# Scan stage: the mean square of a head as two split products in place of one unsplit product

## The reference

```
o = (gla_chunked(q, k_f, v, lf_f)
     + flip_t(gla_chunked(flip_t(q), flip_t(k_b), flip_t(v), flip_t(lf_b))))
o = rmsnorm(o, norm_g.reshape(HG_HEADS, HG_VAL_DIM)).reshape(bsz, t, HG_W).astype(u.dtype)
o = o * jax.nn.silu(gate)
return jnp.concatenate([o, memory_cross_attn(xq, mem_kv)], axis=-1) @ w_out
```

## Time and profile before

| | |
|---|---|
| runs | 1357.15, 1355.12, 1357.15 us, median 1357.15 |
| profiled execution | 1358.22 us, of which the span from first to last instruction is 1356.9 |
| mean granted TensorE clock | 0.996 of full |
| scan stage loop | about 1009 to 1161 us of the span |
| busy: PE / PEld / DVE / ACT / POOL | 98% / 86% / 75% / 58% / 11% |

### The profile page before, as it was taken

How to read it: one execution, slowest core, us unless ns; L and a number is a source line. 1 busy time by engine, 2 the same in 40 slices (tenths; PEclk the granted TensorE clock), 3 DMA queues, 4 the chain that set the end, 5 groups by cost and what they waited for, 6 DMA issues and landing times. The chain is left out here.

```text
span 1356.9 us, 20744 instructions
## 1 busy us (share of the span) xinstructions
PE 1334.4 (98%) x8197; PEld 1160.9 (86%) x8197; DVE 1023.1 (75%) x1670; ACT 785.7 (58%) x1274; POOL 145.0 (11%) x131
## 2 busy tenths in 40 slices
PE   8999999999999999999999999999999999999998
PEld 7887888888898888887987888888789998888887
DVE  5875588777897787778788677766657997786766
ACT  6654266655442566563687565555557785655553
POOL 4760300000100000000000000000303224000000
PEclk9999999999999999999999999999999999999999
DMA  8722355654563456552643255555344435355551
GB/s 304 244 85 119 111 200 217 234 188 184 194 249 125 186 188 251 195 197 101 234 147 119 112 205 199 225 196 187 135 179 153 149 138 189 146 187 205 194 197 70
DMA packets 38607, 242.18 MB, mean 178 GB/s; under 512 B 4448, under 2 KB 7408, under 8 KB 11120
## 3 DMA queue, kind: packets, MB, share of 16 engines
q1 hardware_dynamic: 38512, 240.87, 48.2%
HBM read 236.89 MB, written 2.64 MB: 177 GB/s over the span
## 5 line engine op out<-in xcount | busy, mean ns | idle before, releaser
L320 DVE TENSOR_TENSOR wlo<-raw,whi 128x2048 fp32r<-128x2048 f32 (+1 forms) x179 | 401.2, 2246 | 103.8 <-ACT whi L297 101.7
L297 ACT ACTIVATE whi<-raw 128x2048 fp32r<-128x2048 f32 x195 | 370.4, 1903 | 81.3 <-PE ps L472 40.0
L409 PE MATMUL ps<-XS,whi 128*128 128x512 f32 x1392 | 331.7, 390 | 0.0
L409 PEld LDWEIGHTS ps<-XS,whi 128*128 128x128 f32 x1392 | 257.9, 188 | 52.0 <-issue 0.6
L461 PE MATMUL ps<-whi,MS 128*128 128x512 f32 x960 | 233.5, 391 | 0.0
L461 PEld LDWEIGHTS ps<-whi,MS 128*128 128x128 f32 x960 | 177.5, 188 | 35.8 <-issue 0.4
L414 PEld LDWEIGHTS ps<-XS,wlo 128*128 128x128 f32 x1392 | 178.5, 191 | 6.8
L414 PE MATMUL ps<-XS,wlo 128*128 128x256 f32 x1392 | 180.6, 283 | 0.0
L389 PE MATMUL ps<-XS,whi 128*128 128x256 f32 x672 | 167.8, 289 | 0.0
L390 PE MATMUL ps<-XS,whi 128*128 128x256 f32 x672 | 164.1, 284 | 0.0
L1563 ACT ACTIVATE ar<-ps 128x256 f32<-128x256 f32 x176 | 57.3, 377 | 146.3 <-PE ps L414 146.1
(11 more groups left out here) (328 smaller groups left out, 1548.4 us busy)
## 6 DMA issues: line engine op xcount, KB each, us to landing
raw<-in_up SPq DMA_DIRECT2D x88, 1024.0 KB, 4.8
raw<-in_down SPq DMA_DIRECT2D x44, 1024.0 KB, 4.9
raw<-in_hg_t SPq DMA_DIRECT2D x16, 1024.0 KB, 4.8
raw<-in_od_t SPq DMA_DIRECT2D x8, 1024.0 KB, 5.2
raw<-in_ev_a SPq DMA_DIRECT2D x6, 1024.0 KB, 10.0
raw<-in_wa_o SPq DMA_DIRECT2D x6, 1024.0 KB, 4.9
raw<-in_hg_o SPq DMA_DIRECT2D x6, 1024.0 KB, 4.8
raw<-in_ev_o SPq DMA_DIRECT2D x4, 1024.0 KB, 6.8
```

Of the source, the lines that this page charges most:

```text
L297: ac.activation(parts_of(m)[0][:, 0:w], raw[m % NRAW][:, 0:w], ACT.Copy).then_inc(w_hi)
L320: ve.tensor_tensor(lo[:, c], r[:, c], hi[:, c].bitcast(F32), ALU.subtract).then_inc(w_lo_v)
L409: pe.matmul(banks[i][:, 0:512], hi[:, c], XS[:, k, 0:512], start=(k == 0), stop=False)
```

## The change

The squares of heads 0 to 6 are summed in split form. ScalarE makes the high part of the square, VectorE the low part; they use chunk 7 of `MS`. The matrix of ones is copied once into chunk 6 in the float32r format. TensorE then makes two products where it made one. Head 7 stays as before. In TensorE's order the squares of head n-2 come behind the scores of head n-1. Square also waits until the low part of the head before is made.

```
+        h_one, h_sh, h_sl = mark("h_one"), mark("h_sh"), mark("h_sl")
+        ONES, SRS = MS[:, 6, 0:128], MS[:, 7, :]
...
+                if 0 <= n - 1 < 8:
+                    scores_pe(n - 1)
                 if 0 <= n - 2 < 8:
                     squares_pe(n - 2)
-                if 0 <= n - 1 < 8:
-                    scores_pe(n - 1)
...
         def squares_pe(h):
-            pe.wait_ge(h_sr.sem, h + 1)
             if h:
                 pe.wait_ge(h_rs.sem, h)
-            pe.matmul(HSUM[:, 0:256], C("ones")[:, 0:128], SR, start=True, stop=True).then_inc(h_su.up())
+            if h == 7:
+                pe.wait_ge(h_sr.sem, h + 1)
+                pe.matmul(HSUM[:, 0:256], C("ones")[:, 0:128], SR, start=True, stop=True).then_inc(h_su.up())
+                return
+            pe.wait_ge(h_one.sem, 1)
+            pe.wait_ge(h_sh.sem, h + 1)
+            pe.matmul(HSUM[:, 0:256], ONES, SRS[:, 0:256], start=True, stop=False)
+            pe.wait_ge(h_sl.sem, h + 1)
+            pe.matmul(HSUM[:, 0:256], ONES, SRS[:, 256:512], start=False, stop=True).then_inc(h_su.up())
...
+            ac.activation(ONES, C("ones")[:, 0:128], ACT.Copy).then_inc(h_one.up())
             act_weights(at_z(1))
...
                     if h:
                         ac.wait_ge(h_su.sem, h)
+                        ac.wait_ge(h_sl.sem, h)
                     ac.activation(SR, HVAL[:, 0:256], ACT.Square).then_inc(h_sr.up())
+                    if h < 7:
+                        ac.wait_ge(h_sr.sem, h + 1)
+                        ac.activation(SRS[:, 0:256], SR, ACT.Copy).then_inc(h_sh.up())
...
                     ve.scalar_tensor_tensor(UG[h % 2], HVAL[:, 0:256], col("bng", h), GT[h % 2], ALU.mult,
                                             ALU.mult).then_inc(h_ug.up())
+                    if h < 7:
+                        ve.wait_ge(h_sh.sem, h + 1)
+                        ve.tensor_tensor(SRS[:, 256:512], SR, SRS[:, 0:256].bitcast(F32), ALU.subtract).then_inc(h_sl.up())
```

## The result

The changed kernel's median is 1362.98 us (6 runs, 1361.76 to 1364.85), the kernel before's 1356.24. The ratio is 1.0049, 95% interval 1.0038 to 1.0059: 6.7 us slower (5.2 to 8.0). A second series gave 1.0043 (1.0029 to 1.0057). The profiled execution took 1363.35 us, span 1361.9, against 1358.22 and 1356.9: 5.1 us longer.

A forecast was written before the change was run, and what follows sets the result against it. The prediction took the ScalarE–VectorE ring, not TensorE, to bound the scan stage. It summed 1.15 + 1.9 + 0.58 = 3.6 us to a median of 1360.8 us (profiled 1361.8), 80% range 1357.6 to 1363.2.

The forecast's parts named there:

- What bounds the stage: Scan stage: ScalarE and VectorE waiting on each other set its end at 14.70 us a turn, not TensorE at 14.44.
- The ring: Scan stage: ScalarE and VectorE wait for each other in turn; a turn of 14.70 us was to become 15.08.
- Step 2: First scan step with a low part: it takes VectorE's turn beside GpSimd, L320 ends later; shift 1.15 us, bounds 0.1 to 1.45.
- Five turns: Scan steps 3 to 7: the low part delays L533 and the next exponentials by 0.38 us each, 1.9 us in all.
- Behind the last scores: Step 8: head 6's low part and two products now follow the last scores, adding 0.58 us, bounds 0.24 to 1.5.
- rival (d): Step 8's stall lowers TensorE's clock, or L533 and L320 lose further GpSimd turns: median 1362.5 us; chance 0.09.
- the likeliest: Whole kernel: the main forecast, 3.6 us slower, median 1360.8 us, own range 1359.2 to 1362.6; chance 0.55.
- Turns of 15.1: Sign in the scan: exponentials of steps 4 to 7 start 15.1 us apart, not 14.7.
- a stand of 1 to 2 us ahead of the last scores: Sign at step 8: TensorE newly waits 1 to 2 us before the last scores.
- (a): Scan stage: TensorE is the bound after all and its saved 2.0 us show, 1355.1 us; chance 0.11.
- (b): Step 2 stays clear of GpSimd, so the growth is 2.6 us, 1359.8 us; chance 0.13.
- (c): Scan turns: most growth is given back as scores come earlier; about 1 us in all, 1358 us; chance 0.12.

The follow-up runs named there:

- Square as high part: Changed kernel without the low part of the square and without ScalarE's copy, the Square writing the high part itself: ratio 1.0013.
- high part only: Changed kernel with the low part of the square left out of the sum, ScalarE's copy kept: 1359.80 us, ratio 1.0022.
- Head 0 unsplit: Changed kernel with the squares of head 0 left unsplit, so step 2 has no low part: ratio 1.0022.
- reordered kernels: Three kernels with ScalarE's and VectorE's operations reordered: kernel before, ratio 0.9996; changed kernel, 1.0025; changed kernel without low part, Square writing the high part, 0.9989.

## Why the prediction was right or wrong

**What bounds the stage: right.** The ring of ScalarE and VectorE sets the end. TensorE lost 0.32 us of work per head in two kernels with the ring's old or greater length (Square as high part, high part only), and neither became faster. The saving of the split itself is 0.20 us a head, not the 0.29 forecast, which changed nothing in the sum.

**Step 2, 1.15 us: right**, 1.1 measured, and by the stated way: GpSimd takes the turn behind the low part and L320 runs over 2 us. The rule that the prediction quotes from the Trainium skill, "SBUF — State Buffer", section "Who interferes with whom", held here: L2514, with two inputs in SBUF, took 0.95 us beside GpSimd's operation instead of 0.42. Head 0 unsplit takes the loss away.

**Five turns, 5 x 0.38 = 1.9 us: 2.3 measured, and the step gives the wrong owner.** The prediction had both chains, low part to +1.20 and MS copy to +1.15, and charged VectorE's low part. The MS copy does end at +1.14, but L533 starts 0.10 behind that, at +1.24, an interval for which the prediction had nothing. So the MS copy, delayed by ScalarE's new copy, holds L533. With the low part gone the turns stay at 15.17, and only with ScalarE's copy also out of the way are they 14.73. That the size came out near is luck: the two chains differ by 0.05. That the low part alone would lengthen the ring in this order, to about 15.1, follows from +1.20 and was not run. The excess of 0.08 a turn: L533 starts 0.04 later than forecast, and GpSimd's pair takes 3.47 to 3.53 instead of 3.46.

**Behind the last scores, 0.58 us: 0.46 at full clock** (7.46 against 7.00), but 1.8 in the profile. The difference is rival (d), the clock behind the stand, to which I gave 0.09 together with further lost turns. Its size of up to 1.7 us was about right; that it would fall on top of the forecast in both profiles of the changed kernel was not foreseen.

**The sum** was 3.6 for the profiled execution and 5.1 came. The mis-sized terms are the ring (0.4) and the clock (1.4), less 0.1 behind the scores and 0.2 by which the scan began sooner. The medians differ by 1.6 us more than the profiles. The profile before, with half clock at 43 us and in the norm stage, lay above all six of its runs, while the changed kernel's, with half clock in step 8 and in the norm stage, lay among its own. The forecast of 1360.8 was 2.2 us short, 0.4 beyond the likeliest's own range. The measured 1362.98 is within the 80% range only by what was allowed for rival (d), and as a growth 6.7 us is nearly twice 3.6. So the step that fell short is the clock, which the sum of the likeliest had at nothing.

**What was to show it.** Turns of 15.1 (15.17), a stand of 1 to 2 us ahead of the last scores (1.88) and L320 over 2 us came. TensorE's busy time did not fall by 2 us but rose: the half clock adds to it behind the scores, and ahead of them it is the same at full clock although the work is less. Busy time is a poor sign where an engine waits in short stretches. TensorE's waits from step 5 on are at the scores, for the factors, 0.4 to 0.5 us each; at the squares its weight load waited at most 0.2.

Rivals (a), (b) and (c) are out: the turns grew, step 2 met GpSimd, and nothing was given back but 0.3 us at step 3.

## What to carry to other kernels

An engine that is 98% busy can still be one that waits elsewhere: look for the ring of waits and time one turn of it before valuing work that is taken off the busy engine. Where two chains reach the same operation within a few hundredths, removing the earlier one shows nothing; look at which releaser remains, and try an exchange in the order, which costs no work. A saving on the waiting engine only lengthens its stand, and a stand may cost clock on top, so compare the granted clocks of the timed executions, too.

## What the runs showed of the hardware

- A VectorE operation between two SBUF tiles and a GpSimd tile operation took turns where they met in the rows here: one added operation of 0.42 us in step 2 cost 1.4 us, since the operation behind it lost its turn. In the reordered kernels one of 0.42 took 0.86 to 1.10.
- After 1.9 us without work TensorE ran 3.4 us at 1.2 GHz in both profiles of the changed kernel, beginning 0.8 and 1.3 us behind the stand, and in none of six other profiles with such a stand; 16 needless products of 1.9 us in that gap shortened "scores to values" by 1.36 us.
- VectorE's L533 started 0.10 us behind the end of the ScalarE copy it waited for (changed kernel, high part only), a tenth that decides between two chains here.
- The same kernel's profiles differ by 1.5 us by whether the half clock falls into the norm stage; two profiles alone can't settle a change of 0.1%.
